# A two-block transformer kernel: orders of instructions changed in the query panel's place, the norms, the first attention and the state scan

## The reference, cut to what matters

```
block 1:  h = rms_norm(x) * (1 + sc1) + sh1              # modulation from silu(c) @ ada_w
          q, k, v, f, conv = h @ w_in                    # 8 heads of 64, 512 channels of convolution
          attn = softmax(q k' / 8 + cum[t] - cum[s]) v   # causal, in blocks of 128 queries
          u = silu(layer_norm(causal_conv31(val * sigmoid(gate))))
          x = x + g1 * rms_norm([attn, u] @ w_o)
          h = rms_norm(x) * (1 + sc2) + sh2
          x = x + g2 * rms_norm((silu(h @ w_g) * (h @ w_u)) @ w_ffn_out)
block 2:  state-space mixer (4 chunks of 128 tokens, 32 heads, 4 groups):
          y = scores * decay @ x_chunk + C @ state;  state = state * decay + x_chunk @ B
          y = rms_norm_by_group((y + d * x) * silu(z));  x = x + gate * (y @ w_out)
          k, v = mod(x) @ kv_w;  q, z = mod'(x) @ w      # 16 heads of 64
          a = exp(log sigmoid(logit) + sum of log sigmoid(-logit) after it)   # stick breaking, causal
          x = x + gate * ((a @ v) * silu(z)) @ w_out;  out = rms_norm(x)
```

## Time and profile before

| | us |
|---|---|
| median of 3 runs (lowest, highest) | 1438.09 (1435.17, 1441.22) |
| profiled execution, whole time | 1437.19 |
| its span | 1435.4 |
| PE busy | 1360.9 (95%) |
| DVE busy | 823.6 (57%) |
| ACT busy | 588.3 (41%) |
| POOL busy | 405.6 (28%) |
| mean granted TensorE clock | 0.97 |

### The profile page before, as it was taken

How to read it: one execution, slowest core, us unless ns; L and a number is a source line. 1 busy time by engine, 2 the same in 40 slices (tenths; PEclk the granted TensorE clock), 3 DMA queues, 4 the chain that set the end, 5 groups by cost and what they waited for, 6 DMA issues and landing times. The chain is left out here.

```text
span 1435.4 us, 19530 instructions
## 1 busy us (share of the span) xinstructions
PE 1360.9 (95%) x7904; PEld 1078.1 (75%) x7904; DVE 823.6 (57%) x965; ACT 588.3 (41%) x848; POOL 405.6 (28%) x191
## 2 busy tenths in 40 slices
PE   5999999889999999999999999988998999999996
PEld 3777867668888888887788876766776898777774
DVE  3789853476655544333757556677733822466544
ACT  4323656333222222112444456776522422455451
POOL 0000000039987887998100000000000050233310
PEclk9999999989999999999799999999999999999998
DMA  9433061215454455553222243333122432110121
GB/s 384 160 134 132 30 235 63 84 34 210 177 194 180 171 218 191 190 191 147 92 89 88 96 126 89 118 118 133 59 102 86 151 132 89 59 60 30 59 89 59
DMA packets 41350, 181.12 MB, mean 126 GB/s; under 512 B 3392, under 2 KB 20160, under 8 KB 21312
## 3 DMA queue, kind: packets, MB, share of 16 engines
q1 hardware_dynamic: 40128, 171.73, 33.2%
q10 hardware_dynamic: 1152, 8.39, 1.7%
HBM read 173.75 MB, written 6.36 MB: 125 GB/s over the span
## 5 line engine op out<-in xcount | busy, mean ns | idle before, releaser
L193 DVE TENSOR_TENSOR wlo<-raw,whi 128x2048 fp32r<-128x2048 f32 x95 | 260.8, 2745 | 183.1 <-ACT whi L189 180.6
L200 POOL TENSOR_TENSOR ada_raw<-ada_raw,cs 128x2048 f32<-128x2048 f32 x36 | 142.0, 3944 | 509.6 <-DVE h2lo L451 458.6
L271 PE MATMUL ps<-hhi,whi 128*128 128x512 f32 x640 | 252.0, 394 | 2.4 <-PEq L562 0.8
L271 PE MATMUL ps<-hhi,wlo 128*128 128x512 f32 x640 | 249.4, 390 | 0.0
L271 PE MATMUL ps<-hlo,whi 128*128 128x512 f32 x640 | 249.1, 389 | 0.0
L189 ACT ACTIVATE whi<-raw 128x2048 fp32r<-128x2048 f32 x95 | 181.5, 1911 | 143.6 <-PE ps L1309 91.3
L209 POOL TENSOR_TENSOR ada_raw<-ada_raw 128x1024 f32<-128x1024 f32 x72 | 169.4, 2353 | 5.6
L271 PEld LDWEIGHTS ps<-hhi,whi 128*128 128x128 f32 x640 | 120.2, 188 | 28.6 <-issue 2.4
L271 PEld LDWEIGHTS ps<-hhi,wlo 128*128 128x128 f32 x640 | 120.1, 188 | 25.7
L271 PEld LDWEIGHTS ps<-hlo,whi 128*128 128x128 f32 x640 | 120.3, 188 | 24.3
L2036 POOL TENSOR_TENSOR x<-x,rest 128x256 f32<-128x256 f32 (+3 forms) x32 | 49.0, 1532 | 163.7 <-DVE rest L2331 163.7
(11 more groups left out here) (373 smaller groups left out, 2806.4 us busy)
## 6 DMA issues: line engine op xcount, KB each, us to landing
raw<-panels SPq DMA_DIRECT2D x87, 1024.0 KB, 4.9
ada_raw<-ada SPq DMA_DIRECT2D x48, 1024.0 KB, 6.7
first<-ada SPq DMA_DIRECT2D x8, 1024.0 KB, 19.6
bc<-ac_rows SPq DMA_DIRECT2D x32, 256.0 KB, 3.7
raw<-panels ACTq DMA_DIRECT2D x8, 1024.0 KB, 5.1
x_kept<-x SPq DMA_DIRECT2D x2, 2048.0 KB, 9.6
x<-x_kept SPq DMA_DIRECT2D x2, 2048.0 KB, 8.2
x<-x_in SPq DMA_DIRECT2D x1, 2048.0 KB, 9.3
```

The costliest lines, as they stand in the source:

```text
L193: e.tensor_tensor(wlo[:, c % 2, :, :], raw[:, c % 2, :, :], whi[:, c % 2, :, :].bitcast(F32), ALU.subtract).then_inc(lo_split, 1)
L200: e.tensor_tensor(ada_raw[:, c % 2, :, :], ada_raw[:, c % 2, :, :], cs[:, which, :].unsqueeze(2).to_broadcast([P, KT, 256]), ALU.mult).the ...
L271: mm = e.matmul(ps[:, 2 * (qc % 2) + b, :], w[:, c % 2, 2 * k + b, :], src[part][:, k, :], **flags)
```

## The change

It only moves instructions; no arithmetic is added or left out.

1. `token_sums` come in groups (after banks 3, 5 and 7 and at the end), in both `post_norm`s and in the final norm.
2. In `pre_norm` TensorE waits for the high part of a tile and does its four matmuls with it, then waits for the low part and does the other two. `pre1` and `pre2` get their coefficients earlier on VectorE.
3. First attention: three taps fewer ahead of it, four fewer in unit 0, seven more in units 11 to 14; `ada_keep` of the second rows in units 11 and 12 ahead of `normalise` and `take`; wo panel 13 loaded after matrices 16 to 19; `read_mod` at the head of unit 15.
4. The z quarter between the state products is cut in halves: one between the pairs, one after them.
5. Last chunk: ScalarE's load of an output panel moves from batch 29 to behind `group_squares(1)`; VectorE's split of an output panel moves from group 1 to group 2, and `norm_lo(0)` and `group_rs(1)` from ahead of group 3's output to group 2, ahead of its gate.
6. Second attention: the query panel is j = 7 and the last v panel j = 8. Bank pair 0 is waited for at the first piece of `project`, no more at the first logits; the split of panel c0+10 goes behind unit 0; a tiny Sigmoid after j = 7 loads its table early.

```diff
@@ -299,6 +299,7 @@
   ORDER = [7, 6, 0, 1, 2, 3, 4, 5]
+  SUMS_AFTER = {3: (0, 1, 2), 5: (3, 4), 7: (5, 6)}
@@ -351,11 +352,10 @@
      part(b).then_inc(N["bank_done"] if j < KT - 1 else panels_used, 1)
-     if j == 2:
+     if j == 3:
       pe.wait_ge(*no("kept", 1))
-      token_sums(pe, no, 0, 0, sq, ORDER[0])
-     if j >= 2:
-      token_sums(pe, no, 0, j - 1, sq, ORDER[0])
+     for t in SUMS_AFTER.get(j, ()):
+      token_sums(pe, no, 0, t, sq, ORDER[0])
@@ -471,12 +471,13 @@
     for k in range(k0, k1):
-     pe.wait_ge(*no("lo_ready", k + 1))
-     for b in range(2):
-      for n, (w, part) in enumerate(PASSES):
-       mm = pe.matmul(ps[:, 2 * (qc % 2) + b, :], w[:, c % 2, 2 * k + b, :],
-          (thi, tlo)[part][:, k, :], start=(k == 0 and n == 0),
-          stop=(k == KT - 1 and n == 2), skip_group_check=True)
+     for part, weights in ((0, (whi, wlo)), (1, (whi,))):
+      pe.wait_ge(*no("lo_ready" if part else "hi_ready", k + 1))
+      for b in range(2):
+       for w in weights:
+        mm = pe.matmul(ps[:, 2 * (qc % 2) + b, :], w[:, c % 2, 2 * k + b, :],
+           (thi, tlo)[part][:, k, :], start=(k == 0 and part == 0 and w is whi),
+           stop=(k == KT - 1 and part == 1), skip_group_check=True)
@@ -714,8 +715,8 @@
 
-    DENSE_TAPS = [11, 11, 11, 9, 5, 10, 2]
-    UNIT_TAPS = [5] * 11 + [2, 4, 4, 0, 0]
+    DENSE_TAPS = [11, 11, 11, 9, 5, 9, 0]
+    UNIT_TAPS = [1] + [5] * 10 + [4, 5, 6, 2, 0]
@@ -747,7 +748,7 @@
       order = ["w4", "w5", "w6", "a10", "a11", "w7", "w8", "w9", "w10", "a12", "a13", "w11", "w12", "a14", "a15",
-        "w13", "a16", "a17", "a18", "a19", "a20", "a21", "w14", "w15", "w16", "w17"]
+        "a16", "a17", "a18", "a19", "w13", "a20", "a21", "w14", "w15", "w16", "w17"]
@@ -1048,6 +1049,8 @@
         ins.then_inc(A["exp"], 1)
+       if n in (11, 12):
+        ada_keep(act, ROWS_AT[n][1], MODB, 256)
@@ -1058,7 +1061,7 @@
         take(n - 2)
-       if n in ROWS_AT:
+       if n in (13, 14):
@@ -1151,6 +1154,8 @@
       for n in range(NU + 3):
+       if n == 15:
+        read_mod(dve, 8, 20)
@@ -1162,8 +1167,6 @@
         split_lo(dve, SPLIT_AT[n], 0)
-       if n == 15:
-        read_mod(dve, 8, 20)
@@ -1196,8 +1199,8 @@
       dve.sem_inc(pair_free[1], 2)
+      pre1["coefs"](dve)
       post1["dve"](dve)
-      pre1["coefs"](dve)
@@ -1285,9 +1288,9 @@
       post2["coefs"](dve)
+      pre2["coefs"](dve)
       post2["dve"](dve)
-      pre2["coefs"](dve)
@@ -1488,19 +1491,19 @@
 
-      def z_quarter(k):
+      def z_quarter(k, k2=(0, 4)):
        cp, qp = c0 + p, q0 + p
-       if k % 4 == 0:
+       if k % 4 == 0 and k2[0] == 0:
         pe.wait_ge(pair_free[qp % 2], qp // 2 + 1)
-       for kt in range(k0, k0 + 4):
+       for kt in range(k0 + k2[0], k0 + k2[1]):
             stop=(kt == KT - 1 and j == 2))
-       if k % 4 == 3:
+       if k % 4 == 3 and k2[1] == 4:
@@ -1592,13 +1595,13 @@
          if g == 2:
-          for k in LAYING_OUT[c + 1][0:1]:
-           z_quarter(k)
+          z_quarter(LAYING_OUT[c + 1][0], (0, 2))
            stop=True).then_inc(M["st"], 1)
+        z_quarter(LAYING_OUT[c + 1][0], (2, 4))
@@ -1746,7 +1749,7 @@
          taken += 1
-        for p in taken_at(n - 5) if n >= 5 else ():
+        for p in taken_at(n - 5) if 5 <= n < NN - 3 else ():
@@ -1757,6 +1760,8 @@
       group_squares(1)
+      for p in taken_at(NN - NB):
+       load_panel(act, c0 + p + 4, 0)
@@ -1889,9 +1894,6 @@
            split_lo(dve, c0 + p + 2, 0)
-        if c == TB - 1 and g == MG - 1:
-         norm_lo(dve, 0)
-         group_rs(dve, 1)
@@ -1909,6 +1911,11 @@
           group_rs(dve, 0)
+          for n in range(c * NB, NN - 3):
+           for p in taken_at(n):
+            split_lo(dve, c0 + p + 2, 0)
+          norm_lo(dve, 0)
+          group_rs(dve, 1)
@@ -1918,10 +1925,6 @@
          gate_part(dve, g)
-         if g == 1:
-          for n in range(c * NB, NN - 3):
-           for p in taken_at(n):
-            split_lo(dve, c0 + p + 2, 0)
@@ -1993,6 +1996,8 @@
 
+    if j in (7, 8):
+     return c0 + 15 - j
@@ -2040,9 +2045,9 @@
      for j in range(1, 9):
-      if j == 8:
+      if j == 7:
        pre4["all_low"](pe)
-      in_panel(pe, c0 + j, q0 + j, 0, (h2hi, h2lo) if j == 8 else (hhi, hlo), 4 <= j < 8)
+      in_panel(pe, c0 + j, q0 + j, 0, (h2hi, h2lo) if j == 7 else (hhi, hlo), j in (4, 5, 6, 8))
@@ -2052,7 +2057,6 @@
       if n == 0:
-       pe.wait_ge(pair_free[0], (q0 + 8) // 2 + 2)
@@ -2101,6 +2105,8 @@
         pe.wait_ge(lo_split, c + 1)
+       if mh == 0:
+        pe.wait_ge(pair_free[0], (q0 + 8) // 2 + 2)
@@ -2184,12 +2190,9 @@
       mm.then_inc(nsem["bank_done"] if j < KT - 1 else panels_used, 1)
-      if j == 2:
-       token_sums(pe, fin, 0, 0, fsq, ORDER[0])
-      if j >= 3:
-       token_sums(pe, fin, 0, j - 2, fsq, ORDER[0])
-     for j in range(KT - 2, KT):
-      token_sums(pe, fin, 0, j, fsq, ORDER[0])
+      for t in SUMS_AFTER.get(j, ()):
+       token_sums(pe, fin, 0, t, fsq, ORDER[0])
+     token_sums(pe, fin, 0, KT - 1, fsq, ORDER[0])
@@ -2199,8 +2202,8 @@
       bank = ps[:, 2 * pair:2 * pair + 2, :]
-      if 4 <= j < 8:
-       r = j - 4
+      if j in (4, 5, 6, 8):
+       r = min(j - 4, 3)
@@ -2208,7 +2211,10 @@
        act.activation(qhi[:, 0:2, :], bank, ACT.Copy, scale=scale).then_inc(B["qhi"], 1)
-      split_hi(act, c0 + j + 2, 0)
+      if j < 8:
+       split_hi(act, c0 + j + 2, 0)
+      if j == 7:
+       act.activation(warm[:, 7:8], ones[:, 0:1], ACT.Sigmoid)
@@ -2250,6 +2256,8 @@
           scale=-1.0).then_inc(B["keep"], 1)
+      if n == 0:
+       split_hi(act, c0 + 10, 0)
@@ -2281,12 +2289,13 @@
            ALU.subtract).then_inc(pair_free[pair], 1)
-      elif j == 8:
+      elif j == 7:
              op1=ALU.subtract).then_inc(pair_free[pair], 1)
-      split_lo(dve, c0 + j + 2, 0)
+      if j < 8:
+       split_lo(dve, c0 + j + 2, 0)
@@ -2331,6 +2340,8 @@
        scan.then_inc(B["rest"], 1)
+      if n == 0:
+       split_lo(dve, c0 + 10, 0)
```

## The result

The changed kernel takes 1414.7 us (median of 4 runs, 1412.6 to 1419.6) beside 1438.7 for the kernel before (4 runs): a ratio of 0.984, 95% interval 0.9805 to 0.9875. The forecast was 1416. The profiled execution took 1412.9, its span is 1411.1 us against 1435.4.

What follows compares the result with a forecast made beforehand. TensorE, busy 95% of the span, bounds the kernel, so only its waits, low clock and turns count. Seven terms sum to 22.3 us: 1437.2 becomes 1414.9, plus 0.9 for the median: 1416, 8-in-10 range 1406 to 1428.

Steps and rivals of the forecast that it cites:

- Part 1: First attention, units 0 to 2: fewer early taps remove unit 2's 2.40 us wait and 1.6 of low clock; 4.0 us.
- Rival A: VectorE becomes the bound in the first attention, so removed waits return one unit on; 1422 us, chance 0.15.
- Part 2: First attention, units 11 to 15: earlier ada_keep, matrix transfers and bank 4 read shorten TensorE's waits; 4.5 us.
- the stretch at 195.4: Low clock from 195.40 to 202.20 in the first attention: counted as nothing, up to 3.0 us if it went.
- The step on the transfers: Units 11 and following: removing the 1.13 wait counted 0.5, since matrices land late; the 1.15 transfer wait counted in full.
- Parts 3 and 4: Norms: grouped token sums save turns between product kinds, 3.4 us; high parts first start pre norms sooner, 2.2 us.
- rival B: The clock gives nothing back: low stretches stay, one more follows the wait for group 3's squares; 1422 us, chance 0.13.
- Part 5: Between chunks: six matmuls behind the last product cover the 0.79 us wait for VectorE's copy, three times; 2.1 us.
- Part 6: Last chunk: first output matmul 6.2 us sooner, new wait of 3 to 4 at group 3's squares; gain 2.3 us.
- Part 7: Second attention: logits start with the last v matmul, unit 1's logits come at 1220.55 instead of 1224.33; 3.8 us.
- Rival C: The full yield: the low clock at 195.40 goes and the last chunk gives 3.2; 1412 us, chance 0.10.
- D: Slower: the last chunk's new wait drops the clock through the output panels, up to 1493 us; chance 0.03.

Runs made afterwards that it cites:

- odd: Kernel before plus only the moved taps, grouped sums, the z quarter's half behind the state products and the query panel's new place: 1424.7 us, ratio 0.9918.
- even: Kernel before plus only ada_keep first, w13 behind a19, early read_mod, high parts first with early coefficients, and the last-chunk edits: 1427.9 us, ratio 0.9932.
- fill: Changed kernel plus extra products, results unread, in the first post norm, ahead of pre1, pre2, pre3 and the spread ending the state-space stage: 1413.2 us, ratio 0.9819.
- keep_load: Kernel before with two ScalarE edits alone: ada_keep ahead of the normalisation in units 11 and 12, last-chunk panel loads behind the group's squares: 1433.6 us, one run.
- no_keep: Kernel before with panel w13 behind matrix 19 and bank 4's read at the head of unit 15, without the earlier ada_keep: 1435.5 us, one run.
- vector_back: Changed kernel with VectorE's old order in the last chunk, ScalarE's moved load kept: 1413.4 us, ratio 0.9832.
- squares_later: Changed kernel with group 3's squares' sums one tile later in TensorE's order and their spread at tile 2 of panel 2: 1421.8 us, ratio 0.9891.

## Why the prediction was right, and where it was not

The time was right by 1.3 us and the direction safe, but by terms that were off on both sides. That they cancel in part is luck.

1. *Part 1, 4.0: 4.1 measured, and the same in* `odd`. The taps put back in units 11 to 14 cost nothing. Its 1.6 us of clock, though, is what three of the four traces with that wait have: in `even` the same wait cost 2.40 and nothing more. Rival A, that a wait taken out here is found again one unit on, didn't come true: from unit 3 to unit 11 the lead stays at 3.8 us.
2. *Part 2, 4.5: 6.1.* The mis-sized term is the stretch at 195.4, counted as nothing. It is gone and was worth about the 3.0 that stood beside it as the other reading. The step on the transfers failed the other way: the waits of 1.13 and 1.15 became 0.54 and 0.96, a net 0.8 where 1.65 was forecast. Unit 15 gave 2.2 against 2.8: the walk ended with the normalisation, and the copy behind it in ScalarE's queue ends 0.5 us later (216.52 and 217.01). How firm the 3.0 is, the other traces tell: with all of part 2 the stretch is absent in seven of eight traces (present in `fill`, 6.8 us, behind a wait of 1.70 for a transfer; one of the seven, `even`, has 3.4 us of low clock a unit later), without all of it present in four of four. The changed kernel's trace is the best of its kind, though: in the seven with parts 1 and 2 the stage gives 2.2 to 6.1, 5.1 in the mean. The work in it, transposes and all, is the same in every one. So the rule that was weighed (the Trainium skill, TensorE: Matmul & The Clock Gate, Part 4: PE-mode transpose) doesn't decide here; the measurement does, and by it the low clock went with part 2 as a whole. Through which of its edits, and whether through the waits, isn't shown: `keep_load` has only waits of 0.84 and 0.47 us there and is low, `even` has 0.88 and 1.75 and is not, and there is one trace of each. Open too is why `even` waits 4.25 us for transfers, where the other seven wait 1.5 to 2.6.
3. *Parts 3 and 4 around the norms of block 1, 3.6: 2.0.* The orders did what was said: by their first spreads the post norms had gained 1.3 and 1.2, and pre1's first product follows the first high part. What failed is that the low clock was treated as given. Its stretch in the first norm lasted 3.4 us longer after, and from those spreads to the norms' ends -0.1 and -0.5 us came in, where 1.1 and 0.3 had been added for `pre1` and `pre2`. In that much rival B was right. The longer stretch is not the change's doing, however: `keep_load` and `no_keep`, whose norms are those of before, have 20.5 us of it too, and lose 0.6 and 1.1 us on that way against the trace of before. On the same way and against the same trace the five kernels with the new order and no extra products lose 0.1 to 0.4, the three with the old one (`odd` beside these two) 0.6 to 1.1. So the order gives about 0.6 of its 1.1, and the rest of the miss lies in the one trace that the forecast started from. At pre3 it went the other way: 0.8 from the order and 0.9 because the spread ahead of it ran at the full clock (1.16 us against 2.08). Here the trace of before was an unlucky one: it is low for 10.2 us, and `odd`, `keep_load` and `no_keep`, with this stage as before, are low for 6.8 and gain 0.8 to 1.3 us in it without an edit.
4. *Part 5, 2.1: 2.9.* The turn that was charged is not there; the wait of 0.79 and a little more came back at each boundary.
5. *Part 6, 2.3 (bounds 0 and 3.5): 4.0.* The step trusted least, and above its own bound. Its mechanism held: 6.5 us sooner at the first output product against 6.2, and 2.90 of wait at the squares against 3 to 4. Gate 3 came 4.0 us sooner and not 3.1, and the low clock behind the new wait lasted 3.4 us where 6.8 us had gone from the chunk's end. What the walk missed altogether is which edit mattered: ScalarE's load alone gives the stage, VectorE's new order nothing.
6. *Part 7, 3.8: 3.5.* Unit 1's logits come 4.24 us after the last v product and not 3.9. Its edits were not tried apart.
7. *The tail, 0: -0.8.* The final spread took 2.08 us instead of 1.16: the low clock begins with it at 1400.4, and behind it in the trace before. This too is chance: `keep_load` and `odd` lose the same 0.8 there, `no_keep` and `vector_back` nothing.

The errors, 1.6, 1.7, 0.8 and 0.8 up and 1.6, 0.8, 0.3 and 0.3 down, leave 1.9 of gain more than forecast, and the median moved with it by 1.3. In four of them (part 2, the norms of block 1, pre3, the tail) the clock has the largest share, and one execution's trace can't size these. Rival C's mechanisms (the stretch at 195.4, the whole of the last chunk) came true, beside B's in the norms, and D's low clock past 1035 didn't.

## What to carry to other kernels

Before a wait is taken away, look at what else is late behind it: `squares_later` moved a wait of 2.9 us and met one of 5.8 for another engine in its place, while moving both gave 5 us in the trace. A change to one engine's order should be tried without its companions, since here one moved load did the work of a part with three edits. In a stage where TensorE waits for other engines again and again, small products whose results nobody reads can bring back what the low clock costs: the whole of it in the first norm, a part in the second. They must add to their bank, and each group has to be shorter than the wait it stands in; where there was no wait, at the low clock, five groups took 2.36 us and left 1.3 of it lost. And before a gain of 1 us is read from two traces, look at a third whose edits lie elsewhere: it shows what the stage does by itself.

## What was not expected of the hardware

The same wait doesn't bring the same clock. The wait of 2.40 us in unit 2 stands in four traces: behind it the clock is low for 3.4 us in three of them, and not at all in `even`. The one of 2.37 us ahead of the second attention was followed by 3.4, 3.4, 6.8 and 0 us of low clock (before, `no_keep`, `keep_load`, `even`). The Trainium skill (TensorE: Matmul & The Clock Gate, Part 1: The HAM clock gate) says of the slow start that it is run-variable, with different numbers of slow products for one kernel, and these traces show as much of waits inside a kernel. A term of the clock is thus a mean over such outcomes: by 0.47 us for each us of low clock, about 1.2 us at the first place and 1.6 at the second, with 0 to 3.2 for a single trace.

That `fill` took the sums along agrees with the Trainium skill (PSUM — Partial Sum Buffer, The four PSUM rules): a product that starts a group clears the marks of its whole bank in its partitions, other columns too. The products that add were free of this and cost the same time.
